# Differential attention beside an output projection: each head's values move ahead of the last six matmul passes of the projection's tile in their step

## What is computed

```python
def block(args):
    ...
    logits = jnp.einsum('bqhcd,bkhcd->bhcqk', q_blk, k,
                        preferred_element_type=jnp.float32) * scale
    logits = logits + bias[None, :, None]
    logits = jnp.where(rel[None, None, None] <= 0, logits, -jnp.inf)
    p = jax.nn.softmax(logits, axis=-1)
    w = p[:, :, 0] - lam * p[:, :, 1]
    return jnp.einsum('bhqk,bkhe->bqhe', w.astype(v.dtype), v,
                      preferred_element_type=jnp.float32)
...
o = diff_attention(q, k, v, lam, rel_bias)
o = o * lax.rsqrt(jnp.mean(o * o, axis=-1, keepdims=True) + EPS)
y_attn = (o.astype(h.dtype) * subln_w * (1.0 - lambda_init)).reshape(bsz, seqlen, DA_WIDTH)
return jnp.concatenate([y_ssd, y_attn], axis=-1) @ w_out
```

## Time and profile before

| | us |
|---|---|
| median of 3 runs | 2143.49 |
| lowest, highest | 2142.79, 2143.98 |
| the profiled execution: its own time | 2143.98 |
| the profiled execution: span, first to last instruction | 2142.2 |
| PE busy in that span | 2121.9 (99%) |
| POOL, DVE, ACT busy | 1126.1, 828.7, 805.9 |

### The profile page before, as it was taken

How to read it: one execution, slowest core, us unless ns; L and a number is a source line. 1 busy time by engine, 2 the same in 40 slices (tenths; PEclk the granted TensorE clock), 3 DMA queues, 4 the chain that set the end, 5 groups by cost and what they waited for, 6 DMA issues and landing times.

```text
span 2142.2 us, 29242 instructions
## 1 busy us (share of the span) xinstructions
PE 2121.9 (99%) x10170; PEld 1746.4 (82%) x10170; DVE 828.7 (39%) x1472; ACT 805.9 (38%) x1345; POOL 1126.1 (53%) x1493
## 2 busy tenths in 40 slices
PE   9999999999999999999999999999999999999999
PEld 6888888878887778878888888888787888888887
DVE  5222211763832766143322222217744474023245
ACT  5222232325824645323322233226554343122233
POOL 6555555673354238715655555544645466555554
PEclk9999999999999999999999999999999999999999
DMA  5333333233332223412333233331222223333322
GB/s 207 123 98 98 98 108 106 81 98 99 110 98 79 74 64 120 146 40 89 108 98 95 93 106 99 100 97 60 85 83 79 89 80 100 106 99 98 99 89 79
DMA packets 61344, 207.71 MB, mean 97 GB/s; under 512 B 6616, under 2 KB 8088, under 8 KB 61256
## 3 DMA queue, kind: packets, MB, share of 16 engines
q1 hardware_dynamic: 55216, 195.84, 28.5%
q10 hardware_dynamic: 6040, 10.65, 1.5%
HBM read 204.31 MB, written 4.77 MB: 98 GB/s over the span
## 4 chain that ended last, share of the span: by engine, by line
PE 42%; issue 28%; POOL 27%; DVE 2%; POOLq 0%; ACT 0%; DMA 0%; SPq 0%; DVEq 0%; ACTq 0%
POOL w_lo L463 27%; PE bank L516 11%; PE bank L518 11%; PE bank L517 11%; PE bank L678 1%; PE bank L680 1%; PE bank L679 1%; PE bank L909 1%; PE bank L933 1%; PE bank L841 1%; PE bank L921 0%; DVE gx_lo L2377 0%; DVE bank L2386 0%; PE bank L847 0%; DMA x<-xT 0%
## 5 line engine op out<-in xcount | busy, mean ns | idle before, releaser
L463 POOL TENSOR_TENSOR w_lo<-w_raw,w_hi 128x256 fp32r<-128x256 f32 x1448 | 1092.7, 788 | 936.6 <-ACT w_hi L1284 936.3
L516 PE MATMUL bank<-gx_hi,w_hi 128*128 128x512 f32 (+1 forms) x1768 | 675.0, 382 | 8.6 <-DVE gx_lo L2377 4.5
L518 PE MATMUL bank<-gx_hi,w_lo 128*128 128x512 f32 (+1 forms) x1768 | 668.0, 378 | 0.0
L517 PE MATMUL bank<-gx_lo,w_hi 128*128 128x512 f32 (+1 forms) x1768 | 667.5, 378 | 0.0
L1284 ACT CAST w_hi<-w_raw 128x1024 fp32r<-128x1024 f32 x364 | 379.8, 1047 | 355.3 <-PE bank L518 298.3
L516 PEld LDWEIGHTS bank<-gx_hi,w_hi 128*128 128x128 f32 x1768 | 332.6, 188 | 75.0 <-DVE gx_lo L2377 6.4
L518 PEld LDWEIGHTS bank<-gx_hi,w_lo 128*128 128x128 f32 x1768 | 332.6, 188 | 62.2
L517 PEld LDWEIGHTS bank<-gx_lo,w_hi 128*128 128x128 f32 x1768 | 332.8, 188 | 60.6 <-issue 0.2
L516 PE MATMUL bank<-ff_hi,w_hi 128*128 128x512 f32 x352 | 136.9, 389 | 0.0
L517 PE MATMUL bank<-ff_lo,w_hi 128*128 128x512 f32 x352 | 136.9, 389 | 0.0
L518 PE MATMUL bank<-ff_hi,w_lo 128*128 128x512 f32 x352 | 136.9, 389 | 0.0
(11 more groups left out here) (354 smaller groups left out, 2717.9 us busy)
## 6 DMA issues: line engine op xcount, KB each, us to landing
w_raw<-wstream SPq DMA_DIRECT2D x364, 512.0 KB, 3.5
bias_spread<-bias_rows ACTq DMA_DIRECT2D x1, 2560.0 KB
square<-cum_rows ACTq DMA_DIRECT2D x8, 256.0 KB, 3.7
rfin_row<-cum_rows ACTq DMA_DIRECT2D x8, 256.0 KB, 3.1
outT<-ple_o SPq DMA_DIRECT2D x8, 256.0 KB, 2.0
x<-xT SPq DMA_DIRECT2D x3, 512.0 KB, 8.5
square<-bias_spread ACTq DMA_DIRECT2D x4, 256.0 KB, 2.7
rfin_row<-bias_spread ACTq DMA_DIRECT2D x4, 256.0 KB, 2.8
```

The lines of the kernel that those rows point to most:

```text
L463: ins = nc.gpsimd.tensor_tensor(w_lo[:, s, part], w_raw[:, s, part], w_hi[:, s, part].bitcast(F32), ALU.subtract)
L516: nc.tensor.matmul(dst, hi, rhs[0], start=first, stop=False)
L517: nc.tensor.matmul(dst, hi, rhs[1], start=False, stop=False)
L518: return nc.tensor.matmul(dst, lo, rhs[0], start=False, stop=last)
```

## The change

In the loop of the eight steps on PE, `values(h - 1)` is issued before `ssd_part(h, range(6, 8))` instead of after it. Nothing else differs: neither the instructions nor what they wait for, and the orders on DVE, ACT, POOL and SP are the same.

```diff
@@ -982,9 +982,9 @@
                 scores(h, 3)
                 if h > 1:
                     turn_o(h - 2)
-                ssd_part(h, range(6, 8))
                 if h > 0:
                     values(h - 1)
+                ssd_part(h, range(6, 8))
             attn_chunk(0)
             turn(AH - 1)
             attn_chunk(1)
```

## The result

| | before | changed |
|---|---|---|
| median, us | 2143.38 (6 runs) | 2152.92 (6 runs) |
| lowest, highest | 2142.79, 2143.98 | 2152.10, 2153.33 |
| profiled execution: own time, span | 2143.98, 2142.2 | 2153.33, 2151.5 |

The ratio is 1.0043, with a 95% interval of 1.0033 to 1.0054. The six runs of the kernel before are the three of the table further up and three more. The change costs 9.5 us; 2152.5 was forecast.

The account below looks back on a forecast made before the run. PE and DVE were taken to reach each turn together, with PE nearly always busy. Terms 0.80 + 6.35 + 1.83 = 8.98 us on the profiled 2143.98 gave 2152.96, or 2152.5 against the median; range 2149.5 to 2155.9.

Parts of the forecast that it names:

- Both chains arrive at the turn together: At each turn, PE and DVE finish together; delaying DVE's copy by more than its 0.88 us of idle delays PE.
- Values, 2.15 ahead of the passes: On PE, the values issued ahead make the six passes start 2.15 us later.
- PE's own length, term 0: On PE, scores come at 720.57 against 720.61 us, so PE neither gains nor loses by itself: 0.
- The addition and DVE's queue, 5 x 1.27: Steps 2 to 6: late addition stands ahead of DVE's copy; 2.15 less 0.88 idle delays each turn 1.27 us, 6.35 altogether.
- the low bound: Low end of the cost: idle times worth 0.08 us more each gives 8.4; step 7's wait covered as well, 6.7.
- Step 1, 0.80: Step 1, no low part queued: 2.15 plus 0.19 wait for `w_T`, less 1.54 idle, costs 0.80 us.
- Step 7, 1.83: Step 7, DVE's combination stands ahead of the copy: 2.15 less 0.32 slack at the turn costs 1.83 us.
- The sum, 8.98: Whole kernel: 0.80 for step 1, 6.35 for steps 2 to 6, 1.83 for step 7, together 8.98 us.
- paid once: Rival: DVE is shifted once against PE, then steps stay 12.67 us; 3.1 us in all, 2146.6; chance 0.05.
- Not slower: Rival: DVE's wait for the values decides and goes, with PE's 2.3 us at the turn: 2141.2; chance 0.04.
- `w_T` was not late in steps 2 to 7: Rival: `w_T` copies end after the transposes, so PE waits in these steps; up to 7.3 us more, 2159.8; chance 0.05.
- The clock stayed at 1.00: Rival: PE's new waits at seven turns lower the clock, up to 28 us more, 2181; chance 0.03.

Follow-up runs that it names:

- Experiments 5 to 7: Kernel before, with values issued ahead of the six passes only in step 7 (2145.04 us), only in step 4 (2144.56), in steps 3 and 5 (2145.46).
- experiment 1: Changed kernel with DVE's order turned round too, low part and copy of the values first, addition last: 2143.44 us, ratio 0.9999 to the kernel before.
- two-step run: Kernel before, with values issued ahead of the six passes only in steps 3 and 5: 2145.46 us, ratio 1.0010.
- experiment 5: Kernel before, with values issued ahead of the six passes only in step 7: 2145.04 us, ratio 1.0007.
- experiments 1 to 4: Changed kernel with DVE's addition last 2143.44 us, only copy ahead of addition 2148.63, values ahead of three passes 2152.23; kernel before with addition last 2146.37.

## Why the prediction was right

- **Both chains arrive at the turn together** was the reading on which all rests. Experiments 5 to 7 confirm it: a delay on DVE reaches PE whole, in the step in which it arises.
- **Values, 2.15 ahead of the passes:** 2.15 (716.66 to 718.81).
- **PE's own length, term 0:** 4.20 from transposes to scores in both, and experiment 1 puts the price of the whole order at the 0.22 us of step 1.
- **The addition and DVE's queue, 5 x 1.27:** the steps are 1.26 longer (13.93 against 12.67). Two small errors cancel in this: the addition comes 2.24 later relative to its turn (8.36 against 6.12), since the values start 0.49 behind the transposes and not 0.41, and the low part is followed 0.65 behind its start by the copy though its record lasts 0.74, which makes the old idle time worth 0.09 more than its row says (the low bound had allowed for 0.08). So that 1.27 came out to the hundredth is luck; each of the two terms was off by 0.09.
- **Step 1, 0.80:** 0.77, with the same cancelling: the addition comes 2.41 later relative to its turn (8.14 against 5.73) where 2.34 was put, and the idle time of 1.54 is worth 1.62. The wait for `w_T` in it, put at 0.19, is 0.18 by experiment 1.
- **Step 7, 1.83:** 1.92, the same 0.09 for the addition.
- **The sum, 8.98:** 0.77 + 5 x 1.26 + 1.92 = 8.99 between first and last turn (from 699.06 to 793.95, against 700.08 to 785.98). The medians differ by 9.5; the profiled executions differ by 9.35, of which the attention has 8.99. Outside it, the first turn comes 1.02 sooner in the changed one, whose first scores are 1.03 sooner already (688.00 against 689.03), so ahead of every place that the change touches; the rest after the last turn takes 1.3 longer. For the last see below. That the whole-kernel number came so close therefore rests on these two nearly cancelling as well; the mechanism rests on the 8.99.
- **The rivals:** "paid once" fell with the two-step run. "Not slower" needed the copy to start when the values end; experiment 1 gives DVE that order, and the rival's price comes true there, as far as no loss goes: 2143.44, without the 2.3 that it hoped to win. `w_T` was not late in steps 2 to 7: the list of waits has one wait for it, step 1's. The clock stayed at 1.00 in the attention, with waits of up to 1.8 us for the matmuls of a turn and the ten transposes behind them. The Trainium skill (TensorE: Matmul & The Clock Gate, Part 4: PE-mode transpose) says that the full clock doesn't engage for transposes; here they were not seen to bring it down.

## What to carry to other kernels

When a product is issued earlier, look at the queue of the engine that takes it up: there it may stand behind an instruction that waits for just the work that was overtaken. Then nothing is gained, and everything behind that instruction is late by the length of the work that was moved ahead (here 2.15 us, not the 1.5 of the six passes it overtook), less the idle time that stood behind that instruction before (here 0.88). Move the pair together, producer's order and consumer's order, or neither; and where two engines meet at one instruction with no slack, take the price per round and multiply it by the rounds.

## What the runs showed that was not expected

The granted clock fell in a place that the change doesn't touch, in some executions and not in others. The view of stretches of the changed kernel, around the split norm behind the second block's output projection (`o2`):

```profile
1726.00:1728.00 2.00, 1.25 (x9) 1.14 (x9) 1.48 (x5) 1.36 (x2) 0.78 (x2) 1.00 0.42 123
1728.00:1730.00 2.00, 1.11 (x5) 1.02 (x5) 1.97 (x5) 0.99 (x3) 2.00 (x3) 0.72 0.60 225
...
1732.00:1734.00 2.00, 2.00 (x10) 2.00 (x11) 1.72 (x5) 0.93 (x3) 1.71 (x3) 0.50 0.78 252
```

And of the kernel before, the same place, 8 us earlier in its span:

```profile
1718.00:1720.00 2.00, 1.13 (x9) 1.13 (x9) 1.48 (x5) 1.35 (x2) 0.81 (x1) 1.00 0.53 147
1720.00:1722.00 2.00, 1.11 (x9) 0.91 (x8) 1.97 (x5) 0.88 (x3) 1.97 (x3) 1.00 0.66 231
...
1724.00:1726.00 2.00, 1.25 (x10) 1.25 (x11) 1.97 (x5) 1.23 (x3) 1.71 (x3) 1.00 0.82 242
```

In both, PE is busy for only 1.1 to 1.3 of 2 us in two such stretches. Its waits there are the same in both, 1.08 us for POOL's `w_lo` and 0.89 us for DVE's `gx_lo`. In the one the clock then goes to 0.50, that is 1.2 of 2.4 GHz, for nearly 7 us in all (0.72, 0.50, 0.50 and 0.58 in four stretches of 2 us); in the other it stays at 1.00. The Trainium skill (TensorE: Matmul & The Clock Gate, HAM oscillation — how this bites in real kernels) says that idle gaps between bursts of matmuls let the clock fall. It speaks of longer gaps than these, so this place agrees in kind only; and it is a place in which the clock may fall, not one in which it must. Of the ten kernels' profiled executions three have the fall, all in this place: the changed kernel's, that of experiment 1 (mean clock 0.999) and that of experiment 5 (0.998). It depends on the execution: of the kernel before, on the chip of experiments 1 to 4, 17 runs had a mean clock of 1.000 and a median of 2143.36, 3 had 0.999 and 2143.86, and 6 had 0.998 and 2144.81; on the other chip 19 had 1.000 and 2142.86, 7 had 0.999 and 2143.45, and 5 had 0.998 and 2145.05. So the runs with the deeper fall are 1.5 to 2.2 us slower, which is more than one changed step costs. It is about half of the scatter: all runs spread over 2.8 and 2.6 us on the two chips, those with 1.000 over 1.4 and 1.0. That the runs without a profile had their fall in this same place is likely and not shown. The profiled execution of the changed kernel has it and the one of before has not, which may be the 1.3 us that the end of the former took longer: the 16 instructions of DVE's L2386 on `y_o2` there go from 1716.6 to 1746.3, 29.7 us, against 28.2 before (1708.7 to 1736.9). Taking only runs with a clock of 1.000, the changed kernel is at 2152.65 (4 runs) and the kernel before on the two later chips at 2143.36 and 2142.86.
